# Attention probabilities copied by DMA to a second buffer, and three of four transposed as float32r

## What is computed

```python
def one_block(qblk):                      # 128 queries at a time
    sc = jnp.einsum('bqkgd,bskd->bkgqs', qblk, k).astype(jnp.float32) * scale
    p = jax.nn.softmax(sc, axis=-1).astype(v.dtype)
    return jnp.einsum('bkgqs,bskd->bqkgd', p, v)
```

## Time and profile before

| | us |
|---|---|
| median of three runs | 1083.92 |
| the profiled execution, its own time | 1086.1 |
| its span (first to last instruction) | 1083.7 |
| projection, about | 0 to 149 |
| attention, about | 149 to 395 |
| output projection, routing | 395 to 520 |
| experts | 520 to 1084 |

### The profile page before, as it was taken

How to read it: one execution, slowest core, us unless ns; L and a number is a source line. 1 busy time by engine, 2 the same in 40 slices (tenths; PEclk the granted TensorE clock), 3 DMA queues, 4 the chain that set the end, 5 groups by cost and what they waited for, 6 DMA issues and landing times.

```text
span 1083.7 us, 16970 instructions
## 1 busy us (share of the span) xinstructions
PE 1044.8 (96%) x5689; PEld 896.7 (83%) x5689; DVE 886.0 (82%) x1147; ACT 775.3 (72%) x1095; POOL 423.3 (39%) x394
## 2 busy tenths in 40 slices
PE   8999999999999999998699999999999999999995
PEld 7999978999889987887578888888888888888884
DVE  6787669989999843338899999999999999999991
ACT  7655569888998843344577877877878878788771
POOL 2466576111358502334524432344323444234101
PEclk9999999999999999999799999999999999999998
DMA  8232050010211348741799999999999999999982
GB/s 305 79 116 102 1 197 1 2 41 20 98 41 40 98 109 263 225 164 79 235 417 378 398 400 400 400 421 400 401 400 400 413 408 401 400 400 406 415 310 39
DMA packets 77936, 266.05 MB, mean 245 GB/s; under 512 B 11249, under 2 KB 13516, under 8 KB 77628
## 3 DMA queue, kind: packets, MB, share of 16 engines
q1 hardware_dynamic: 69776, 239.68, 56.9%
q0 software_dynamic: 8048, 25.68, 8.3%
q10 hardware_dynamic: 60, 0.01, 0.0%
HBM read 239.07 MB, written 26.28 MB: 245 GB/s over the span
## 4 chain that ended last, share of the span: by engine, by line
PE 48%; DVE 2%; DMA 1%; issue 1%; ACT 0%; POOLq 0%; POOL 0%; DVEq 0%; ACTq 0%
PE ps L2003 10%; PE ps L2005 10%; PE ps L2004 10%; PE ps L2017 5%; PE ps L2019 5%; PE ps L2018 5%; PE ps L1980 1%; DMA xe<-h,idxT 1%; DMA out<-y,give 1%; DVE lo L2171 0%; DVE idx L1776 0%; DVE affT L1785 0%; DVE gates L1771 0%; ACT hi L2093 0%; POOLq L2274 0%
## 5 line engine op out<-in xcount | busy, mean ns | idle before, releaser
L2171 DVE TENSOR_TENSOR lo<-raw,hi 128x2048 fp32r<-128x2048 f32 x191 | 430.0, 2285 | 32.3 <-ACT hi L2093 32.0
L2093 ACT ACTIVATE hi<-raw 128x2048 fp32r<-128x2048 f32 x192 | 364.6, 1918 | 70.0 <-PE ps L2005 57.3
L2003 PE MATMUL ps<-hi,xehi 128*128 128x512 f32 x480 | 188.3, 392 | 1.3 <-DVE h L2193 1.0
L2005 PE MATMUL ps<-hi,xelo 128*128 128x512 f32 x480 | 186.9, 389 | 0.0
L2004 PE MATMUL ps<-lo,xehi 128*128 128x512 f32 x480 | 186.8, 389 | 0.0
L1939 POOL DMA_INDIRECT xe<-h,take x60 | 111.1, 1851 | 25.1 <-issue 13.7
L2003 PEld LDWEIGHTS ps<-hi,xehi 128*128 128x128 f32 x480 | 90.1, 188 | 20.2 <-issue 1.4
L2005 PEld LDWEIGHTS ps<-hi,xelo 128*128 128x128 f32 x480 | 90.1, 188 | 18.8
L2004 PEld LDWEIGHTS ps<-lo,xehi 128*128 128x128 f32 x480 | 90.2, 188 | 18.1
L1934 POOL COPY take<-idx 128x4 uint32 (+1 forms) x15 | 29.0, 1930 | 193.7 <-DVE xt L2187 187.4
L1361 DVE TENSOR_TENSOR probTlo<-ps,probThi 128x512 fp32r<-128x512 f32 x128 | 87.8, 686 | 12.1 <-ACT probThi L1318 10.0
(11 more groups left out here) (302 smaller groups left out, 2192.3 us busy)
## 6 DMA issues: line engine op xcount, KB each, us to landing
raw<-in_w_down SPq DMA_DIRECT2D x64, 1024.0 KB, 10.0
raw<-in_w_gate SPq DMA_DIRECT2D x60, 1024.0 KB, 9.7
raw<-in_w_up SPq DMA_DIRECT2D x60, 1024.0 KB, 9.3
w_raw<-in_w_in SPq DMA_DIRECT2D x8, 592.0 KB, 9.0
x<-in_x SPq DMA_DIRECT2D x8, 512.0 KB, 3.7
woraw<-in_w_o SPq DMA_DIRECT2D x4, 1024.0 KB, 5.1
o<-attention_out SPq DMA_DIRECT2D x8, 512.0 KB, 4.4
xr<-in_x SPq DMA_DIRECT2D x8, 512.0 KB, 7.0
```

The costliest lines, as they stand in the source:

```text
L2003: pe.matmul(ps[:, dst[n], :], rowhi[:, c, :], hi[w][:, cols], start=c == 0, stop=False)
L2005: last = pe.matmul(ps[:, dst[n], :], rowlo[:, c, :], hi[w][:, cols], start=False, stop=c == KD - 1)
L2093: act.activation(hi[s][:], raw[s][:], ACT.Copy).then_inc(hi_done, 1)
L2171: dve.tensor_tensor(lo[s][:], raw[s][:], hi[s][:].bitcast(F32), ALU.subtract).then_inc(lo_done, 1)
```

## The change

A second ring of buffers `turn`, three of 128 x 512, is added. When the exponential of unit v is done, SP copies `prob[v % 3]` to `turn[v % 3]` by a DMA of 256 KB, and TensorE transposes from `turn`. Three of four units of a head (all but the first, whose transposes alternate with `turn_output`) are transposed with data and identity read as float32r; the first stays float32. The transposes come one step later (unit u - 4 in step u), and with them the high and low parts, the value pairs, the output of a head and the tail; `STEPS` is 9. The exponential of unit v now waits for the landing of the copy of unit v - 3. The copies stand in SP's program; the stores of heads, the loads of w_o and of the first rows are placed after the copies of certain units. Semaphores of the weight loads serve again for the copies. The router's weights `wr` move to another place in SBUF.

```diff
@@ -250,6 +250,7 @@
         att["pthi"] = [Map(shared_at)("probThi0", [P, TS, 2 * P], F32R), bm("probThi1", [P, TS, 2 * P], F32R)]
         att["v"] = [bm(f"v{i}", [P, TS, 2, VD], F32R) for i in range(2)]
         att["ot"] = bm("ot", [P, SEQ])
+        att["turn"] = [bm("turn0", [P, SEQ])]
         assert bm.at <= w_in_end, (bm.at, w_in_end)
 
         om = Map(weights_at)
@@ -260,8 +261,8 @@
         om = Map(w_in_end)
         wo["lo"] = om("wolo", [P, KD, D], F32R)
         wo["small"] = om("smallo", [P, 128])
-        wo["wr"] = om("wr", [P, KD, EXPERTS])
         wo["aff"] = [om(f"aff{i}", [P, 64]) for i in range(2)]
+        att["turn"] += [om(f"turn{i}", [P, SEQ]) for i in (1, 2)]
         assert om.at <= end
         om3 = Map(temps_at)
         wo["o"], wo["x"] = [om2("o0", [P, D])], [om2("xr0", [P, D])]
@@ -278,6 +279,7 @@
         assert om3.at <= sq_at
         wo["h2"] = [om3(f"h2_{i}", [P, D]) for i in range(2)]
         wo["gffn"] = om3("gffn", [P, D])
+        wo["wr"] = om3("wr", [P, KD, EXPERTS])
         assert om3.at <= weights_at, (om3.at - weights_at)
 
         mm = Map(arena)
@@ -472,7 +474,7 @@
         steps.did(pool.memset(k["minus_half"][:], -0.5))
         steps.did(pool.memset(k["ident"][:], 0.0))
         steps.wait()
-        pool.affine_select(out=k["ident"][:], in_=k["ident"][:], compare_op=ALU.not_equal, fill=1.0,
+        pool.affine_select(out=k["ident"][:].bitcast(F32R), in_=k["ident"][:], compare_op=ALU.not_equal, fill=1.0,
                            base=0, pattern=[[-1, P]], channel_multiplier=1).then_inc(ident_ready, 1)
         pool.wait_ge(ident_ready, 1)
         pool.tensor_tensor(k["halves"][:], k["ident"][:, 0:VD], k["ident"][:, VD:P], ALU.add).then_inc(halves_ready, 1)
@@ -968,7 +970,8 @@
             row_stats(t)
 
     signals = {"rows_ready": rows_ready, "mla_ready": mla_ready, "kv_done": kv_done, "proj_done": proj_done,
-               "row_copied": row_copied, "halves_ready": halves_ready, "rows_set": rows_set, "pj_back": pj_back, "mla_back": mla_back, "xlo_done": xlo_done, "clo_done": clo_done}
+               "row_copied": row_copied, "halves_ready": halves_ready, "rows_set": rows_set, "pj_back": pj_back, "mla_back": mla_back, "xlo_done": xlo_done, "clo_done": clo_done,
+               "w_loaded": w_loaded}
     return (sync_program, gpsimd_program, tensor_program, scalar_program, vector_program), signals
 
 
@@ -979,8 +982,14 @@
     rows_ready, mla_ready, kv_done, proj_done, row_copied, pj_back, mla_back, xlo_done, clo_done, halves_ready = (
         project_signals[n] for n in ("rows_ready", "mla_ready", "kv_done", "proj_done", "row_copied", "pj_back", "mla_back",
                                      "xlo_done", "clo_done", "halves_ready"))
-    STEPS = 8
+    STEPS = 9
     ALL = SETS * HEADS
+    turn = att["turn"]
+    turn_loaded = project_signals["w_loaded"][0:len(turn)]
+
+    def loaded(v):
+
+        return turn_loaded[v % 3], 16 * (v // 3 + 2)
     units = [(g, i) for g in range(ALL) for i in range(TS)]
     NU = len(units)
     qhi, khi = att["hi"]
@@ -1063,17 +1072,34 @@
             sp.dma_start(o_rows[TS * s:TS * (s + 1), :, cols].rearrange("t p d -> p t d"),
                          att["rows"][s][0][:, :, cols]).then_inc(o_stored, 16)
 
-        for h0, h1 in O_PARTS:
-            store_heads(0, h0, h1)
-        sp.wait_ge(o_stored, 16 * len(O_PARTS))
-        for i in range(KD // 2):
+        def load_output_weights(i):
             if i >= 2:
                 sp.wait_ge(wo_lo, 2 * (i - 1))
             sp.dma_start(wo["raw"][:, 2 * (i % 2):2 * (i % 2) + 2, :],
                          a["w_o"].rearrange("(k p) n -> p k n", p=P)[:, 2 * i:2 * i + 2, :]).then_inc(wo_loaded, 16)
-        route_first(sp)
-        for h0, h1 in O_PARTS[:-1]:
-            store_heads(1, h0, h1)
+
+        def copy_probs(v):
+            sp.wait_ge(exp_done, v + 1)
+            if v >= 3:
+                sp.wait_ge(pt_ready, v - 2)
+            sp.dma_start(turn[v % 3][:], att["p"][v % 3][:]).then_inc(turn_loaded[v % 3], 16)
+
+        for v in range(NU):
+            copy_probs(v)
+            for s, unit in ((0, 0), (1, NU // 2)):
+                for h0, h1 in O_PARTS:
+                    if v == unit + TS * h1 + 10 and v < NU - 1:
+                        store_heads(s, h0, h1)
+            if v == NU // 2 + 13:
+                sp.wait_ge(o_stored, 16 * len(O_PARTS))
+                load_output_weights(0)
+                load_output_weights(1)
+            elif v == NU // 2 + 24:
+                load_output_weights(2)
+            elif v == NU // 2 + 38:
+                load_output_weights(3)
+            elif v == NU - 8:
+                route_first(sp)
         route_second(sp)
         store_heads(1, *O_PARTS[-1])
         route_rest(sp)
@@ -1187,11 +1213,13 @@
 
         def transpose_prob(u, i):
             if i == 0:
-                pe.wait_ge(exp_done, u + 1)
+                pe.wait_ge(*loaded(u))
                 if u >= 2:
                     pe.wait_ge(ptlo_done, u - 1)
             cols = slice(i * P, (i + 1) * P)
-            turned = pe.transpose(ps[:, T_BANKS[u % 2], cols], att["p"][u % 3][:, cols], k["ident"][:])
+            as_type = F32 if u % TS == 0 else F32R
+            turned = pe.transpose(ps[:, T_BANKS[u % 2], cols].bitcast(as_type), turn[u % 3][:, cols].bitcast(as_type),
+                                  k["ident"][:].bitcast(as_type))
             if i == TS - 1:
                 turned.then_inc(pt_ready, 1)
 
@@ -1237,9 +1265,9 @@
                 prepare(kind, g)
             if u < NU:
                 scores(u)
-            pair = (u - 6) // 2 if u >= 6 and u % 2 == 0 and (u - 6) // 2 < PAIRS else None
-            turned = u - 3 if 0 <= u - 3 < NU else None
-            output = (u - 11) // TS if u >= 11 and (u - 11) % TS == 0 else None
+            pair = (u - 7) // 2 if u >= 7 and u % 2 == 1 and (u - 7) // 2 < PAIRS else None
+            turned = u - 4 if 0 <= u - 4 < NU else None
+            output = (u - 12) // TS if u >= 12 and (u - 12) % TS == 0 else None
             for i in range(TS):
                 if output is not None:
                     turn_output(output, i)
@@ -1251,10 +1279,10 @@
                 o_transposes(0, 0)
             elif u == NU:
                 o_transposes(0, 1)
-            elif u == NU + 3:
+            elif u == NU + 4:
                 product(0, 0)
                 product(0, 1)
-            elif u == NU + 4:
+            elif u == NU + 5:
                 product(0, 2)
                 o_transposes(1, 0)
                 product(0, 3)
@@ -1293,8 +1321,8 @@
         rows(T - 1)
         queries(T - 1)
         for u in range(NU + STEPS):
-            if u >= 9 and (u - 9) % TS == 0:
-                g = (u - 9) // TS
+            if u >= 10 and (u - 10) % TS == 0:
+                g = (u - 10) // TS
                 act.wait_ge(pv_done, TS // 2 * (g + 1))
                 if g:
                     act.wait_ge(o_ready, g)
@@ -1305,13 +1333,13 @@
                 v = u - 1
                 act.wait_ge(max_done, v + 1)
                 if v >= 3:
-                    act.wait_ge(pt_ready, v - 2)
+                    act.wait_ge(*loaded(v - 3))
                 act.activation(att["p"][v % 3][:], ps[:, S_BANKS[v % 3], :], ACT.Exp, bias=att["nmax"][:, v:v + 1],
                                accum_out=att["sum"][:, v:v + 1]).then_inc(exp_done, 1)
             if u == 2:
                 keys_values(T - 1)
-            if 0 <= u - 3 < NU:
-                v = u - 3
+            if 0 <= u - 4 < NU:
+                v = u - 4
                 act.wait_ge(pt_ready, v + 1)
                 if v >= 4:
                     act.wait_ge(pv_done, v // 2 - 1)
@@ -1354,8 +1382,8 @@
         prepare("k", 0)
         prepare("q", 0)
         for u in range(NU + STEPS):
-            if 0 <= u - 4 < NU:
-                v = u - 4
+            if 0 <= u - 5 < NU:
+                v = u - 5
                 dve.wait_ge(pthi_done, v + 1)
                 cols = pair_cols(v)
                 dve.tensor_tensor(ptlo[v // 2 % 2][:, :, cols], ps[:, T_BANKS[v % 2], :].rearrange("p (a c) -> p a c", a=TS),
@@ -1366,8 +1394,8 @@
                                   negate=True).then_inc(max_done, 1)
             for kind, g in due.get(u, []):
                 prepare(kind, g)
-            if u >= 11 and (u - 11) % TS == 0:
-                g = (u - 11) // TS
+            if u >= 12 and (u - 12) % TS == 0:
+                g = (u - 12) // TS
                 h = g % HEADS
                 pj, rsum = rows_of(g)[0], att["rsum"][:, g % 2, :]
                 dve.wait_ge(exp_done, TS * (g + 1))
```

## The result

The changed kernel takes 1099.86 us (median of 4 runs, 1096.23 to 1103.48) against 1084.07 for the kernel before run beside it (4 runs, 1083.49 to 1086.82). The ratio is 1.0143, 95% interval 1.0110 to 1.0176: slower by 15.8 us, where 4.5 us faster was forecast, and outside the range given. The profiled execution took 1100.84 us with a span of 1099.0.

A forecast was written before the change was run, and what follows sets the result against it. The prediction took TensorE to bound the attention, with VectorE the next limit. Transposes -11.6, start +4.3, DMAs between copies +2.3 and tail +0.5 gave -4.5 us, from 1083.9 to 1079.4 us, range 1073 to 1093.

The forecast's parts named there:

- The steady state of the copies: Attention away from bulk transfers: each 256 KB copy lands in about 2.3 us within 3.1 us of slack, cost 0.
- The transposes: Probability transposes in attention: float32r takes 0.06 us each instead of 0.11, MLA heads saving 8.8 and GQA heads 2.8: -11.6 us.
- the third rival: Probability transposes: 0.085 us each, half the gain, some 6 us saved; +1 us in all, 1085; chance 0.10.
- The GQA heads: Transpose gain in GQA heads, with VectorE as ceiling at 0.35 us: 0.25 us a head over 11 heads, 2.8 us.
- The start: Start of attention: the first copy waits behind the latent rows' reload on SP's queue, landing at about 159.1: +4.3 us.
- The DMAs between copies: Attention from unit 78 on: w_o loads delay copies and SP waits for POOL's split near unit 120: +2.3 us (0 to 7).
- the pair: Two 1 MB w_o loads after unit 77's copy: unit 78's copy lands at about 7.5 us, 6.2 allowed: +1.3 us.
- The last single load: One of two single w_o loads that hold a copy to about 5 us where 4.7 to 6 is allowed: 0.5 together.
- The tail: End of attention: the last copy needs 2.4 us after an exponential starting about 1 us sooner: +0.5 us (0 to 2).
- the added step "adds none": Attention pipeline: the deeper order moves work to a later step and adds no work, cost 0.
- the second: Rival: in the three plain bursts the stationary load bounds float32r transposes too, gain zero; +7.1 us, 1091; chance 0.18.
- Rivals 4 and 5: Short float32r transpose passes get no discount, 1095 or more, chance 0.06; copies land late throughout, 1096, chance 0.04.

The follow-up runs named there:

- e10_act_copies: The changed kernel, but ScalarE issues every copy on its own queue and SP runs the earlier kernel's order: 1112.72 us, ratio 1.0268 against the kernel before.
- e9_reload_act: The changed kernel, but ScalarE issues the whole reload of the latent rows on its own queue, copies staying on SP's: 1104.26 us, ratio 1.0191 against the kernel before.

## Why the prediction was wrong

- **The steady state of the copies**: right. They land in 2.2 us, and most units don't wait.
- **The transposes, -11.6, measured about -3.4**: 8.2 us missed, enough by itself to turn -4.5 into +3.7. It has two parts. The price: I took 0.06 us, arguing that the load costs no more beside halves; in a row the loads come 0.085 apart, though PE's first starts stand 0.06 apart as I had said they would. That is the price of the third rival, which had given half the gain; the 107 ns worked out, as an estimate, from the rule of the Trainium skill ("TensorE: Matmul & The Clock Gate", LDWEIGHTS) doesn't hold for float32r here, while the float32 loads, 0.108 to 0.112 apart, agree with it. And the base: I read a burst as 0.44 us, by taking 0.12 off for the high product behind it. But the earlier trace rows themselves have that product at 332.94, 0.36 behind the first transpose: the 0.12 of a series is not the product's distance at a change of kind, where 333.14 - 332.94 = 0.20 stands. Of the 0.13 us by which a burst fell short (0.20 forecast, 0.07 measured) the base is 0.08. The GQA heads, 2.8 of the sum, gave nearly none of it.
- **The start, +4.3, measured +5.8**: mechanism and place right. The copy landed at 160.8 instead of 159.1. It does stand behind the reload on SP's queue, as I wrote, but a queue of its own wouldn't have helped: the outstanding bytes hold it (e10_act_copies). The 5.8 is net of 0.9 us that head 0 gains from the added step.
- **The DMAs between copies, +2.3, measured about +13.8** (9.2 and 4.6): the largest miss, 11.5 us, and it too would have turned the sign by itself, to +7.0. For the pair I let the copy land 7.5 us after the pair's issue and allowed 6.2; it landed after 307.07 - 295.26 = 11.8, and the transposes were due after 300.37 - 295.26 = 5.1. The difference is the 6.7 us of the wait. I used the landings of the kernel before, when nothing else was outstanding beside these loads: the pair's later one landed in 10.5 us, not 7. A copy issued 0.5 us ahead and an instruction fetch stood beside it this time; which of them made it later wasn't separated. The upper bound of 7 for this term was too low for the same reason. The last single load, priced at half of 0.5, cost 4.6 in this execution, 3.0 in the wait and about 1.6 in the clock behind it. I had counted the clock at the start and left it out here.
- **The tail, +0.5, measured +1.4** (20.3 against 18.9 us from head 31's first row maximum), of which only 0.32 is a wait for a copy. That the added step "adds none" holds only in sum: it saves about 2 us in heads 0 and 2 and gives 1.4 back here.
- The ledger closes by its own stretches: 0.4 + 5.8 - 3.3 + 9.2 + 4.6 + 0.2 = +16.9 us at the end of the attention, where -4.5 was forecast. No rival had this: the second ended at 1091 on the slow side with the load as its cause, and its stalls were still the 7.1 us, where 5.8 + 13.8 = 19.6 was measured. Rivals 4 and 5 reach 1095 and 1096, by transposes that gain nothing and by copies late throughout, and neither happened.

## What to carry to other kernels

A small DMA that an engine of the critical path waits for is priced by what else is outstanding when it is issued, not by its landing in an idle stretch. Price each meeting with a bulk transfer at the time that transfer still needs, add the clock where TensorE is the bound, and cut the bulk up or move it; another queue didn't help here. The saving of a faster form is best read as the distance from its first instruction to the next instruction of another kind, in the same series, not from the spacing inside another one.

## What the runs showed of the hardware

- A 256 KB copy within SBUF lands in 2.2 to 2.3 us undisturbed, in 3.6 to 4.2 where one 16 KB instruction fetch was under way, in 8.8 to 9.6 behind 2 to 3.6 MB of loads on its own queue, in 8.7 with the same 3.6 MB on another queue, and in 11.6 where that load had been issued only 1.4 to 1.8 us before it, on ScalarE's queue:

```profile
kv_rowsB<-first_kv ACTq DMA_DIRECT2D x1, 2112.0 KB, 12.9
q_rowsB<-first_q ACTq DMA_DIRECT2D x1, 1536.0 KB, 6.4
turn<-prob SPq DMA_DIRECT2D x1, 256.0 KB, 11.6
```

- With bulk and copies on two queues the packets went about one for one (112 and 122 in 156 to 162 us of e9_reload_act), whatever their size (2 and 16 KB).
- A float32r transpose of 128 x 128 in a row starts its load every 0.085 us, a float32 one every 0.110. Between halves the order turns round: 0.305 against 0.285 us from one transpose to the next.
- A pause of about 5.6 us left TensorE at 0.50 of its clock for some 5 us behind it, and this cost only about 0.4 us where VectorE and ScalarE were the next limit. Behind a pause of 3.0 us it cost about 1.6 in an MLA head, where TensorE is the limit.
